# A three-stage encoder kernel: rotary angles moved to VectorE's first weight splits, sine rows kept in DRAM, first and last steps of attention reordered

## Time and profile before

| | us |
|---|---|
| runs shown | 2626.5, 2631.14 (median), 2634.41 |
| the profiled execution, its own time | 2619.49 |
| its span, first to last instruction | 2617.7 |
| mean granted TensorE clock | 0.993 of full |

### The profile page before, as it was taken

One profiled execution on the slowest core, in us unless ns is written; L12 is line 12 of the kernel. 1 busy time (PEld: TensorE's weight loads), 2 busy tenths in 40 slices (PEclk: granted clock), 3 DMA queues, 4 the chain that ended last, 5 costly groups with the idle time before them and its releaser, 6 DMA issues. The chain is left out here.

```text
span 2617.7 us, 48053 instructions
## 1 busy us (share of the span) xinstructions
PE 2554.9 (98%) x17333; PEld 2405.0 (92%) x17333; DVE 1889.0 (72%) x3883; ACT 1450.1 (55%) x3540; POOL 436.5 (17%) x206
## 2 busy tenths in 40 slices
PE   6999999999999999999999999999999999999998
PEld 6899999999999999999999996888999999999787
DVE  5546661129998889898898985788888666666766
ACT  4434322238888888888888881225445445444210
POOL 1000000012454445444444410000000000000000
PEclk8999999999999999999999999999999999999999
DMA  4655454312233434333333316765554543553443
GB/s 156 196 164 190 146 164 123 112 44 51 51 82 83 95 81 97 83 74 80 81 75 90 75 47 181 215 191 176 207 181 171 197 154 129 183 190 137 142 144 112
DMA packets 245281, 337.06 MB, mean 129 GB/s; under 512 B 86386, under 2 KB 182530, under 8 KB 232514
## 3 DMA queue, kind: packets, MB, share of 16 engines
q1 hardware_dynamic: 227218, 325.61, 41.5%
q10 hardware_dynamic: 17840, 8.52, 1.1%
HBM read 224.54 MB, written 108.98 MB: 127 GB/s over the span
## 5 line engine op out<-in xcount | busy, mean ns | idle before, releaser
L1248 DVE TENSOR_TENSOR b_pt_lo<-b_transposed,b_pt_hi 128x384 fp32r<-128x384 f32 (+4 forms) x784 | 429.1, 564 | 49.7 <-ACT b_pt_hi L1141 46.2
L1141 ACT ACTIVATE b_pt_hi<-b_transposed 128x384 fp32r<-128x384 f32 (+4 forms) x784 | 382.3, 502 | 117.3 <-PE b_transposed L1175 108.2
L1128 ACT ACTIVATE ground<-b_ring,ground 128x384 f32<-128x384 f32 (+7 forms) x784 | 436.3, 561 | 19.6 <-DVE ground L1238 11.6
L1233 DVE TENSOR_REDUCE ground<-b_ring 128x1 f32<-128x384 f32 (+7 forms) x784 | 409.7, 528 | 27.6 <-PE b_ring L45 14.8
L1175 PE MATMUL b_transposed<-identity,ground 128*128 128x128 f32 (+2 forms) x2448 | 380.0, 272 | 8.0 <-DVE b_pt_lo L1248 5.0
L1175 PEld LDWEIGHTS b_transposed<-identity,ground 128*128 128x128 f32 (+2 forms) x2448 | 279.8, 134 | 55.7 <-issue 25.4
L43 PE MATMUL b_ring<-region 128*128 128x384 f32 (+7 forms) x784 | 301.2, 384 | 4.1 <-DVE b_transposed L1209 2.4
L43 PE MATMUL p_banks<-p_x_hi,big 128*128 128x258 f32 x896 | 254.3, 284 | 10.2 <-DVE big L581 8.8
L45 PE MATMUL b_ring<-region 128*128 128x384 f32 (+7 forms) x784 | 258.7, 330 | 0.0
L44 PE MATMUL b_ring<-region 128*128 128x384 f32 (+7 forms) x784 | 258.5, 330 | 0.0
L45 PE MATMUL p_banks<-p_x_hi,big 128*128 128x258 f32 x896 | 254.1, 284 | 0.0
(11 more groups left out here) (213 smaller groups left out, 6408.1 us busy)
## 6 DMA issues: line engine op xcount, KB each, us to landing
ground<-x_a SPq DMA_DIRECT2D x23, 1032.0 KB, 5.6
ground<-w_conv SPq DMA_DIRECT2D x32, 512.0 KB, 3.7
c_tiles<-w_conv SPq DMA_DIRECT2D x32, 512.0 KB, 3.9
c_ln<-weight_sums SPq DMA_DIRECT2D x16, 1024.0 KB, 8.0
c_tiles<-weight_sums SPq DMA_DIRECT2D x16, 1024.0 KB, 7.2
weight_sums<-c_tiles SPq DMA_DIRECT2D x9, 1024.0 KB, 3.9
keys<-ground SPq DMA_DIRECT2D x64, 129.0 KB, 5.2
queries<-ground SPq DMA_DIRECT2D x64, 129.0 KB, 2.6
```

The costliest lines, as they stand in the source:

```text
L1128: nc.scalar.activation(p[0:rows, n % PSLOTS, 0:w], banks[0:rows, n % RING, 0:w], ACT.Exp, bias=nmax[0:rows, tile % 8:tile % 8 + 1], accum_ ...
L1141: nc.scalar.activation(turned(pt_hi, g, u, nb)[:, :, tile_columns(u, j)], tb[:, n % 2, 0:nb, 0:rows], ACT.Copy).then_inc(pt_hi_done, 1)
L1233: ins = nc.vector.tensor_reduce(top, bank[0:rows, 0:w], AX, ALU.max, negate=(chunks == 1))
L1248: nc.vector.tensor_tensor(lo, tb[:, n % 2, 0:nb, 0:rows], hi.bitcast(F32), ALU.subtract).then_inc(pt_split, 1)
```

## The change

The angles now stand in four quarters of 516 columns (32 partitions for each quarter), in `rot`, which no one else needs yet. The positions come as one load of 128x516, the constants and gains as one. GpSimd's three passes become VectorE's; the eleven passes are put in three groups between its first weight splits. ScalarE takes two sines of 128x516 (of the angles and, with scale -1, of their negatives) into the upper half of the staging buffer right after its copies of latent 0. SP stores them to a DRAM scratch, waits for that, and loads 16-row pieces back into `rot`: four loads for the rows that the keys need, four for the doubled rows. Takes into that half of the staging buffer wait for the store. The key is rotated without ScalarE (the second product is written to other partitions directly), keys 0 and 1 at the end of VectorE's list of `("o", 0)`, into two alternating rows of 32 partitions; SP stores them after k7. That step's lists are written out anew for both engines. In stage b the clearing of `tb`, the copies and the splits of head 0's values move behind the first scores; TensorE waits for `tb` at its first transpose. In stage cde ScalarE's first `gate_hi` stands ahead of its two DMA issues. The lay-out code for the tables changes to suit.

```diff
-HALF_T = T // 2
+QUARTER = T // 4
...
-        ppos = small[:, 0:4 * CA].bitcast(I32)
-        ang, turns = stage[:, 0:HALF_T], stage[:, HALF_T:T]
+        ppos = small[:, 0:QUARTER].bitcast(I32)
+        ang, turns = (rot[:, n * QUARTER:(n + 1) * QUARTER] for n in range(2))
+        sines = stage[:, T // 2:T].rearrange("p (a t) -> p a t", t=QUARTER)
...
+        def stage_free(eng, r):
+            if STAGE // 2 <= r < STAGE:
+                eng.wait_ge(sines_kept, 16)
+            for s, n in SLOT_AFTER[r]:
+                eng.wait_ge(stored[s], n)
...
+            def turn_tables(to, landed):
+                for at, minus, row in ((0, 0, 0), (16, 0, 0), (64, 0, 16), (80, 1, 16)):
+                    rows = sines_d[minus].rearrange("(q r) t -> r q t", q=4)[row:row + 16]
+                    sp.dma_start(rot[to + at:to + at + 16, :].rearrange("r (q t) -> r q t", q=4), rows).then_inc(landed, 16)
+
+            def store_key(c):
+                sp.wait_ge(k_sum, c + 1)
+                sp.dma_start(kr_d[:, chunk_cols(c)], krs[32 * (c % 2):32 * (c % 2) + 32, :]).then_inc(kr_out[c % 2], 16)
+
...
-            sp.dma_start(rc[:, :], rope_c).then_inc(const_in, 16)
-            sp.dma_start(g_sb[:, :], gains).then_inc(const_in, 16)
+            sp.dma_start(consts[:, :], constants).then_inc(const_in, 16)
+            sp.dma_start(ppos[:, :], pos).then_inc(const_in, 16)
             load_piece(1)
-            for half in range(2):
-                sp.dma_start(ppos[64 * half:64 * half + 64, :], pos[:, half * HALF_T:half * HALF_T + HALF_T].to_broadcast([64, HALF_T])).then_inc(const_in, 16)
...
-                    for c in {0: (), 1: (0, 1)}.get(g, (g,) if g < NCA else ()):
-                        sp.wait_ge(k_sum, c + 1)
-                        sp.dma_start(kr_d[:, chunk_cols(c)], krs[0:32, :]).then_inc(kr_out, 16)
-                    if g == 2:
-                        sp.wait_ge(sined, 4)
-                        sp.dma_start(rot[32:64, :], rot[0:32, :]).then_inc(rot_doubled, 16)
-                        sp.dma_start(rot[96:P, :], rot[64:96, :]).then_inc(rot_doubled, 16)
+                    if g == 1:
+                        sp.wait_ge(sined, 2)
+                        sp.dma_start(sines_d.rearrange("a p t -> p a t"), sines).then_inc(sines_kept, 16)
+                        sp.wait_ge(sines_kept, 16)
+                        turn_tables(0, rot_in)
+                        turn_tables(32, rot_doubled)
+                    if 2 <= g < NCA:
+                        store_key(g)
...
                     store(r)
+                    if kind == "o" and g == 0 and n == PAIRS - 1:
+                        store_key(0)
+                        store_key(1)
...
             copies(0)
+            act.wait_ge(angle, 1)
+            nc.scalar.activation(sines[:, 0], ang, ACT.Sin).then_inc(sined, 1)
+            nc.scalar.activation(sines[:, 1], ang, ACT.Sin, scale=-1.0).then_inc(sined, 1)
             split_weights(PIECES_AT["p", 0])
...
+                    if (kind, g) == ("o", 0):
+                        take(mine[0])
+                        root(1)
+                        take(mine[1])
+                        split_weights(extra)
+                        for r in mine[2:4]:
+                            take(r)
+                        latent(1)
+                        for r in mine[4:]:
+                            take(r)
+                        continue
...
-                for part in (0, 64):
-                    last = nc.vector.tensor_tensor(kt[part:part + 32, :], of[part:part + 32], rot[part:part + 32, chunk_cols(g)], ALU.mult)
-                last.then_inc(k_turned, 1)
-                dve.wait_ge(k_shifted, g + 1)
-                if g:
-                    dve.wait_ge(kr_out, 16 * g)
-                nc.vector.tensor_tensor(krs[0:32, :], kt[0:32, :], ksh[0:32, :], ALU.subtract).then_inc(k_sum, 1)
+                nc.vector.tensor_tensor(kt[0:32, :], of[0:32], rot[0:32, chunk_cols(g)], ALU.mult)
+                nc.vector.tensor_tensor(ksh[0:32, :], of[64:96], rot[64:96, chunk_cols(g)], ALU.mult).then_inc(k_turned, 1)
+                dve.wait_ge(k_turned, g + 2)
+                if g >= 2:
+                    dve.wait_ge(kr_out[g % 2], 16 * (g // 2))
+                nc.vector.tensor_tensor(krs[32 * (g % 2):32 * (g % 2) + 32, :], kt[0:32, :], ksh[0:32, :], ALU.subtract).then_inc(k_sum, 1)
...
             split_half_x0(0)
             split_weights([("x", 0)])
             split_half_x0(1)
+            turns_of_angles()
             split_weights([("x", 1)])
+            angles_within_turn()
             split_weights([("x", 2)])
+            angles_within_pi()
             split_x(1)
...
+                if g == 0:
+                    take(mine[0])
+                    mean_taken(1)
+                    take(mine[1])
+                    newton(1)
+                    split_weights(extra)
+                    take(mine[2])
+                    normalise(1)
+                    take(mine[3])
+                    latent(1)
+                    rotate_key(0)
+                    rotate_key(1)
+                    continue
...
                 if letter == "E":
+                    if n == RING:
+                        nc.scalar.activation(v[:, 0, 1:, 0:VH], raw_v_blocks[:, 1:], ACT.Copy).then_inc(first_hi, 1)
+                        nc.scalar.activation(v[0:META, 0, 0, 0:VH], raw_v_blocks[0:META, 0], ACT.Copy).then_inc(first_hi, 1)
...
+                    if n == 0:
+                        pe.wait_ge(tb_set, 1)
...
                 if letter == "M":
+                    if n == RING:
+                        nc.vector.memset(tb[:, :, :, :], 0.0).then_inc(tb_set, 1)
+                    if n == RING + 3:
+                        dve.wait_ge(first_hi, 2)
+                        nc.vector.tensor_tensor(v[:, 0, 1:, VH:], raw_v_blocks[:, 1:], v[:, 0, 1:, 0:VH].bitcast(F32), ALU.subtract).then_inc(first_split, 1)
+                        nc.vector.tensor_tensor(v[0:META, 0, 0, VH:], raw_v_blocks[0:META, 0], v[0:META, 0, 0, 0:VH].bitcast(F32), ALU.subtract).then_inc(first_split, 1)
...
             act.wait_ge(r_out, 32 * HEADS)
+            gate_hi(0)
             load_sums(act, 1)
-            gate_hi(0)
             gate_hi(1)
```

More of the change, by code:

```diff
@@ L316, in _ @@
                 if kind == "z" and g == KEYS_IN:
-                    sp.wait_ge(kr_out, 16 * NCA)
+                    for n in range(2):
+                        sp.wait_ge(kr_out[n], 16 * (NCA // 2))
                     for s in range(STAGE):
@@ L381, in copies @@
                     nc.scalar.activation(craw[:, j, :], banks[:, j, 0:CA], ACT.Copy).then_inc(c_taken, 1)
-            def shift_key(g):
-                if g < NCA:
-                    act.wait_ge(k_turned, g + 2)
-                    nc.scalar.activation(ksh[0:32, :], kt[64:96, :], ACT.Copy).then_inc(k_shifted, 1)
             def root(g):
@@ L433, in _ @@
                         copies(1)
-                        act.wait_ge(angle, 1)
-                        for half in range(2):
-                            for part in range(2):
-                                nc.scalar.activation(rot[64 * part:64 * part + 32, half * HALF_T:half * HALF_T + HALF_T],
-                                                     ang[64 * half + 32 * part:64 * half + 32 * part + 32, :], ACT.Sin).then_inc(sined, 1)
-                        shift_key(0)
-                        shift_key(1)
                         continue
@@ L679, in _ @@
                         split_x(2)
-                        dve.wait_ge(angle_step, 3)
-                        for part in (TURN1, TURN2, TURN3):
-                            then(nc.vector.scalar_tensor_tensor(ang, turns, -part, ang, ALU.mult, ALU.add))
-                        then(nc.vector.tensor_scalar(ang, ang, rc[:, 2:3], None, ALU.add))
-                        then(nc.vector.tensor_scalar(turns, ang, 1 / TURN, ROUND, ALU.mult, ALU.add))
-                        then(nc.vector.tensor_scalar(turns, turns, -ROUND, -TURN, ALU.add, ALU.mult))
-                        then(nc.vector.tensor_tensor(ang, ang, turns, ALU.add))
-                        nc.vector.tensor_scalar(ang, ang, PI_BELOW, -PI_BELOW, ALU.min, ALU.max).then_inc(angle, 1)
                     else:
@@ L758 @@
 PSLOTS = 14
-Own = namedtuple("Own", "region big_hi big_lo rot work small w_raw x_raw stage means gains rope small_b raw_v o_b o_t p ident stored o_out r_out gate_out meta meta_in")
+Own = namedtuple("Own", "region big_hi big_lo rot work small w_raw x_raw stage means consts small_b raw_v o_b o_t p ident stored o_out r_out gate_out meta meta_in")
 GROUND_P = 2 * P + KKV + KQ + 3
@@ L773, in own_memory @@
     p = arena[:, sum(sizes) - PSLOTS * HALF:].rearrange("p (a b) -> p a b", b=HALF)
-    means, g_sb, rc = (ground[:, sum(sizes) + at:sum(sizes) + to] for at, to in ((0, 2 * P), (2 * P, 2 * P + KKV + KQ), (2 * P + KKV + KQ, GROUND_P)))
```

(12 more changed lines are left out.)

64 lines of the change are left out of this document (29 added, 35 removed).

## The result

Three measurements of the changed kernel gave medians of 2609.55, 2608.85 and 2607.84 us, and the kernel before, run beside them, 2627.86, 2626.78 and 2628.2. The ratios are 0.9924 [0.9907, 0.9942], 0.9932 [0.9917, 0.9947] and 0.9923 [0.991, 0.9937]. So the change is **faster by 18 to 20 us** (0.7 to 0.8%), where 15.7 was forecast. The profiled execution of the changed kernel took 2612.59 (span 2610.8, clock 0.995), 6.9 less than the profiled execution of before.

What follows compares the result with a forecast made beforehand. TensorE, busy 98% of the span, was taken as the bound, leaving only pauses and halved clock. Savings 14.1 - 0.4 + 1.0 + 1.0 = 15.7 gave 2603.8, plus 11.6 offset 2615.4 us; range 2608.5 to 2622.5.

Steps and rivals of the forecast that it cites:

- Part 1: Early projections, 39.79 to 62.38 us: TensorE's long pause, most of a second and halved clock go, 14.1 us saved.
- Part 2: VectorE's eleven shorter angle passes among the first splits, before projection 1: 5.7 to 6.5 us against 6.0 idle, 0.4 lost.
- Part 3: Start of attention: TensorE's first score no longer waits for cleared PSUM, 1.0 us saved, bounds -0.3 and +3.2.
- Part 4: Start of the output stage: ScalarE splits the meta tile before issuing two loads, 1.0 us saved, bounds 0 and 1.15.
- the engine becomes the bound of this stretch: Before projection 1, 9.51 to 20.42 us: the moved passes fill VectorE's 6.0 us of idle time almost exactly, so VectorE bounds.
- the passes cost as much as the old ones: Rival, before projection 1: VectorE ends its split at 24.6, 3.8 us more are lost, total 2619.2; chance 0.17.
- The way through DRAM: SP's store and reload of sines, costed at nothing; rival that it blocks SP loses 32 us, total 2647, chance 0.04.
- The cover is those 7 to 11 us: SP's queue: slack before turned keys (near 45) and x tile 3 (near 49.5) are wanted; beyond it TensorE would pause.
- The clock stays up: Rival, starts of attention and output stage: full clock after the shorter pauses, 2.6 us more gain, total 2612.8; chance 0.17.
- The turned keys are late: Rival, key tile of projection 2: VectorE's second rotation reads the bank late, pause of 1 to 2 us, 2616.9; chance 0.07.
- A change of ScalarE's table costs more than its load: Rival, ScalarE's two early table loads: hidden extra cost makes the root and k0 2 us late, total 2617.4; chance 0.04.
- The carried offset: Whole kernel: the median of the runs shown lay 11.6 us above the profiled execution, added to 2603.8 for the forecast.

Runs made afterwards that it cites:

- only_p: The changed kernel with the starts of stages b and cde as before, so the new stage p alone: 2611.02 us, ratio 0.9946 to the kernel before.
- only_tb: The changed kernel with head 0's value copies and splits back at attention's start, only clearing and its wait moved: 18.5 us from stage p's end to the 81st matmul.
- again: The changed kernel once more, unedited, to see the scatter of traces: 2608.85 us.
- changed_again: The changed kernel once more, unedited, run beside the last experiments: 2607.84 us.
- only_b_c: The kernel before with only the new starts of attention and of the output stage: 2625.27 us, ratio 0.9995 [0.9985, 1.0005].
- keys_first: The changed kernel with keys 0 and 1 rotated in step p 1, ahead of VectorE's first takes: 2613.12 us, ratio 0.9944 to the kernel before.

## Why the prediction was right or wrong

The sign and the main mechanism were right: the pause of stage p and the halved clock behind it went. The size was short. The median of 2609.55 lies 5.9 below the forecast's 2615.4 and below its band of 2611 to 2619, inside its range of 2608.5 to 2622.5. Of the 5.9, 3.3 is the base: the median of the three runs shown was 2631.14, that of the six beside the changed kernel 2627.86. The other 2.6 is the gain, 18.3 by those medians against a sum of 15.7.

The traces say which terms. Measured on five traces of the new stage p and three of the old, the gain stands at 13.2 us at the key tile of projection 2 (63.22 - 50.02), where parts 1 and 2 gave 13.7; at 14.7 at the 605th matmul and 15.2 at the end of stage p, where the sum had put nothing more; with 1.7 for part 3, where it had 1.0, and 1.0 for part 4 that is **17.9**. The five new traces lie 5 us apart at the end of stage p (554.04 to 559.11), so by an estimate from that spread 15.2 is good to about 1 us.

**The steps that failed**: in size, the sum put nothing behind part 1's stretch, where 2.0 came, and 1.0 for part 3, where 1.7 came, beside the base; in mechanism, part 2's "the engine becomes the bound of this stretch", where the landing of a DMA was the bound.

*Part 1, the pause: as forecast.* From k4 to the key tile of projection 2 it took 50.66 - 42.21 = 8.45 us, with 8.5 forecast for this stretch, at full clock and without a pause. The first take of VectorE came at 35.66, not 34, still ahead of its need.

*Part 2, the passes: the price right, the bound wrong.* The eleven passes took 5.95 us (5.7 to 6.5 forecast), so "the passes cost as much as the old ones" fell. But "the engine becomes the bound of this stretch" failed. The forecast let VectorE's list run against a landing of x tile 1 taken from one trace, 16.1, though that landing scatters by 2 us between executions and was the last to come here. Where it did come at 16.1, in only_p, VectorE began its split with no wait and projection 1 started at 20.48 as before: the passes fit, and cost nothing. (The 0.4 lost is no difference of the terms given: 5.7 is less than the cover of 6.0.) In the changed kernel the loss was then not 0.4 but 42.21 - 39.79 = 2.4 in this trace (projection 1 came 1.1 later, the rest is halved clock), -0.2 in only_p, 0.8 in only_tb, 1.2 in again and 4.7 in changed_again, 1.8 in the mean, and decided by a DMA. The range of this term should have been built on that. Whether the new order of loads also delays this one isn't shown: the three old traces have 16.1, 16.2 and 17.0, the new ones with a whole load 15.5 to 18.3; it didn't come sooner, as the lower bound had it.

*Beyond Part 1 I had put nothing.* 1.5 us more came between 62 and 112: the three old traces have a pause of 0.90, 1.23 and 1.94 us before a mean of squares near 90 to 92 (VectorE's line 588), and no new one has it in that place, though two of the five have 0.85 and 0.59 before the 605th. About half of the 1.5 comes from one trace, only_b_c, where the clock was 0.51 from 93 to 96, behind its 1.94. This is the term that the sum lacked. What the traces show of it: ScalarE begins its split of x tile 4, behind which VectorE's own split and then these squares come, 22.8, 23.0 and 23.7 us after the key tile of projection 2 in the old order and 20.5 to 21.7 in the new. Which entry of its list freed it I haven't tried. Another 0.5 came by the end of stage p, less than the traces can tell.

*The way through DRAM: nothing lost, but with far less cover than I gave it.* The store took 6.5 us to land and the last table row 6.9, near what was forecast. "The cover is those 7 to 11 us" was counted for the tables and for x tile 3. The key stores behind them, for which I wrote no need at all, already held ScalarE 0.5 us behind the first value product in the changed kernel, and 8.7 us more cost 6.6 by the end of the stage. keys_first shows the rows' own cover: the fourth landed at 37.86, and a rotation ahead of the first takes waited for it.

*Part 3, start of attention: right in sign, under-sized, and for the wrong reason.* 1.7 instead of 1.0, inside the bounds. I took the earlier score as the gain and held the ninth maximum to be level with before. only_tb shows that the earlier score alone is worth nothing. The ninth maximum came 8.29 after the last matmul of stage p, in only_p 9.49. That the copies and splits of the values, moved behind the fifth and eighth score, fall partly into waits that the engines had there is my reading, and untested. The clock isn't separated from it either, and may be a good part of the 1.7. All four traces with the copies first ran at half clock for some microseconds there (the earlier trace rows for one). Of those with the new start only_b_c, the changed kernel's first and changed_again did not; again did for less long (0.84 from 560 to 570) and took 16.3; keys_first did from 570 to 573 and took 17.1.

*Part 4: as forecast*, 1.0.

*The rivals.* "The clock stays up" came half true: full clock at attention's start (1.00 from 560 to 570, where the earlier trace rows had 0.52), but around the output stage's pause of 2.94 the clock was 0.50 from 1565 to 1571, where the earlier trace rows had 0.59; in changed_again it stayed whole there. "The turned keys are late" did not happen: the second rotation's read of the bank was over at 49.1, and the key tile came at 50.66 without a pause. "A change of ScalarE's table costs more than its load": the loads took 1.28 and the sine began 0.02 after its load. The Trainium skill's drain of 1380 ns (ScalarE: Activation LUTs, "What ACT_TABLE_LOAD costs") isn't seen here either, while its 1283 ns for the load are.

*The carried offset.* The forecast of 2603.8 for an execution of the profiled kind missed by 8.8, since the traced execution of before was 8 us quicker than that kernel's median beside the experiments (2627 to 2629), and the three traced ones of the changed kernel (2612.6, 2612.0, 2616.5) 3 to 9 slower than theirs. The forecast then added 11.6 for the median, where the changed kernel's median lies 3.0 below its profiled execution. Of 8.8 too little and 14.7 too much there stayed 5.9 too much: that 2615.4 came so near is in part luck. The gain is to be taken off the median; the profiled execution gives the terms, not the level.

## What to carry to other kernels

Before a list on one engine is filled up to its idle time, look who ended that idle: where it was a DMA, its landing in several executions is the bound, not the sum of the list, and a pause in front of TensorE may cost more than its length in clock (after 2.73 and 3.69 us some 1.5 and 2.7 more here, after 2.19 nothing). When transfers are put into a queue, count the cover of everything behind them, stores that free a buffer included, and not only of what is loaded. A pause in front of TensorE is worth removing whole: here a second pause and 2.6 us of halved clock went with the long one.

## What the runs showed of the hardware that was not expected

- GpSimd's three scalar passes over 128x516 took 0.78, 1.55 and 2.79 us, and VectorE's product beside the first two took 1.52 instead of 1.23. During the third VectorE stood idle for 1.8 of the 2.79 us, so a busy VectorE isn't what makes that one slow; what does is open.
- Load times of one transfer scatter: x tile 1 (1 MB) landed at 17.2, 17.4 and 18.3 us in three executions of one kernel. From 22 to 26 us the granted clock was 0.54 and 0.60 in the first, 1.00 in the second and 0.50 in the third, where the pauses ahead were 2.73, 2.19 and 3.69. The length of the pause doesn't decide alone: one of 1.21 us at attention's start was followed by a clock of 0.84 from 560 to 570 in again, by 1.00 in the first.
- With the eight row loads and x tile 3 under way, the DMA engines were busy all the time and moved 130 to 163 GB/s (the windows of the changed kernel, below), where from 24 to 26 us they moved 386. x tile 3 took 10.3 us for 1 MB, the next x tile, issued at 57.95, took 6.8.

```profile
34.00:36.00 2.00, 2.00 (x16) 1.89 (x15) 2.00 (x3) 0.39 (x1) 0.00 (x0) 1.00 1.09 163
...
38.00:40.00 2.00, 2.00 (x19) 2.00 (x18) 1.93 (x4) 1.03 (x2) 0.00 (x0) 1.00 1.09 131
```
